# Moving one eighth of a gate projection from slot 11 to slot 19 in the last stick-breaking iteration

## The chip, the cores and the metric

The kernel runs on one core of one Trainium2 chip. The metric is the device time of one execution in microseconds; the time before is the median of 3 runs, 2171.8 us (2169.79 to 2174.42). Less is better.

## The reference, cut to what matters

One decoder layer on 1024 tokens of width 1024, all in float32. After an RMSNorm one input projection feeds two branches and two sigmoid gates:

```python
h = rms_norm(x, norm1_g)
proj = h @ w_in                      # sb_q, sb_k, sb_v, gla_q, gla_k, gla_v, gla_r, gla_lr, gate_sb, gate_gla
# (A) stick-breaking attention, 16 heads x 64, blocks of 128 queries
z = q @ k.T * scale                  # q, k normed per head
log_not = where(mask, log_sigmoid(-z), 0)
w = where(mask, exp(log_sigmoid(z) + reverse_cumsum_after(log_not)), 0)
o_sb = w @ v
# (B) gated linear attention -> o_gla
merged = sigmoid(gate_sb) * (o_sb @ w_branch_sb) + sigmoid(gate_gla) * (o_gla @ w_branch_gla)
x = x + merged @ w_out
x = x + (silu(h2 @ w_ffn_gate) * (h2 @ w_ffn_up)) @ w_ffn_down      # h2 = rms_norm(x)
```

The change is in (A), in its last pair of heads, beside which the last two tiles of 128 gate columns are computed.

## The kernel before, in words

The stages follow each other: norm and transpose, gated linear attention, stick-breaking attention, merging with the output projection, and the feed-forward part. Every float32 product is made of three matmuls of a high and a low part (high by high, low by high, high by low), so each operand is first rounded (`hi`) and the rest is kept (`lo`).

The stick-breaking stage (`stick_breaking`) takes two heads (one pair) in each of 8 iterations. An iteration is written out as 32 slots, and every engine walks the same slots in the same order, each with its own part of a slot's work. The parts meet through counting semaphores; nothing reorders them, so a wait holds all that stands behind it on its engine.

- Scores (`SCORE_SLOT`, 16 of them, n = 0 to 15, slots 0 to 7, 9 and 11 to 17). TensorE makes a block of 128 query rows in `z` (L612 to L615), ScalarE takes two sigmoids of it (L756 `rest`, L757 `beta`), VectorE scans one (L913), GpSimd multiplies the two into `rows` (L526). `rest` and `beta` have two buffers, so the sigmoids of score n wait for GpSimd's product of score n - 2.
- Weights (`WEIGHT_SLOT`, 24 of them, m = 0 to 23, slots 6 to 9 and 11 to 30). TensorE transposes a column of `rows` (L628) into bank `t`, ScalarE rounds it to `wt_hi` (L765), VectorE takes the rest `wt_lo` (L919), and one slot later TensorE multiplies both with `v` into `o` (`weigh`, L641 to L648). From `TAIL_STEP`, m = 13, on (slot 20) the odd m use bank `g0` and the transpose need not wait for the last `wt_lo`. After m = 3, 11, 15 and 23 ScalarE copies half of `o` (L770) and VectorE adds it up (L880); the next m waits for that sum. m = 11 is multiplied in slot 19, so m = 12 waits in slot 20 for the sum.
- Projection (`fill`, L149). A tile of 128 projected columns is made of 8 eighths of 6 matmuls each, four eighths for each half of the tokens. In iterations 1 to 7 a slot takes an eighth in each of the 32 slots. In the last iteration only two gate tiles are left, 16 eighths, and the list `LAST_FILL` gives their slots. After each fourth eighth, in the slot behind it, ScalarE takes the sigmoid of that half (`gate`, L732, into `sb_sq`), and the sync engine (SP) sends it to `gates_t` (L460). GpSimd splits the weight tile of step 6 in slot `LAST_FILL[7] + 2` and that of step 7 in slot `LAST_FILL[15] + 2` (L123 to L127), when the last reader of the buffer is done.
- Branch tiles. From slot 20 (`SPLIT_SLOT`) on, ScalarE and VectorE split one row block of the other branch's output per slot into `h_hi` and `h_lo` (L774, L924), and from slot 22 on TensorE multiplies 6 of them into `z` (L660). The blocks come through a ring of three buffers `og`, loaded by SP (L488), each load after the third waiting for the `h_lo` three blocks back.

SP takes its transfers in one written order. In the last iteration it is: two weight tiles, og blocks 0 to 2, the four gate halves (each waits for its `gate`), four loads `y<-osb_t` (L492), then og blocks 3 to 7 with three more y loads between them, and the output block after the last sum.

In the merging stage TensorE first finishes the last two branch tiles (L1760, `z`), then the eight of the other branch. A barrier stands between the stages.

Of the kernel before, what the change touches and what calls it, by code (L numbers as in the profile page):

```python
# [327 lines left out]
FIRST_UNITS = 4  # L328
LAST_GATES = 2
SB_TILES = FIRST_UNITS + 4 * (PAIRS - 1) + LAST_GATES  # L330
LAST_FILL = list(range(1, 12)) + list(range(14, 19))
TAIL_STEP = 13
MS_SLOT = [6, 10, 13, 17]
MS_AFTER = [10, 13, 17]
# [12 lines left out]
def stick_breaking(nc, c, hT, w_in, qk_gains, osb_t, gates_t, W, following, ot, ot_out, ot_read, ogla_t, z0, y, y_in):  # L347

    with ExitStack() as ctx:
# [75 lines left out]
        def slot_of_unit(s):  # L425
            return s // 8, s % 8
# [5 lines left out]
        with nc.Block() as block:  # L432
# [79 lines left out]
            def _(pool):  # L512
# [16 lines left out]
                def body(it, last):  # L529
# [3 lines left out]
                    if last:  # L533
                        splits = {0: (5, 0), LAST_FILL[7] + 2: (6, 1), LAST_FILL[15] + 2: (7, 2)}
                    else:
# [10 lines left out]
            def _(pe):  # L546
# [3 lines left out]
                def fill(it_units, step, eighth, use):  # L550

                    half, part = eighth // 4, eighth % 4
                    if eighth == 0:
                        W.take(pe, it_units, step)
                    if part == 0:
                        pe.wait_ge(g_free[half], use + 1)
                    ins = project_part(nc, G[half][:], W.tile(step), hT, half, part, 4)
                    if part == 3:
                        ins.then_inc(g_done[half], 1)
# [103 lines left out]
                def body(it, last):  # L663
                    for s in range(SLOTS):
# [9 lines left out]
                        if not last and s in SPREAD_SLOT and s not in SPREAD_AFTER:  # L674
                            spread(SPREAD_SLOT.index(s))
                        at = LAST_FILL.index(s) if last and s in LAST_FILL else s
                        u, eighth = slot_of_unit(at)
                        if s in LAST_FILL if last else u < 4:
                            fill(units(it), FIRST_UNITS + u, eighth, g_uses(it) + (u if last else (0, 2, 5, 6)[u]))
# [17 lines left out]
            def _(act):  # L697
# [30 lines left out]
                def gate(n_done, half, use):  # L728

                    act.wait_ge(g_done[half], use + 1)  # L730
                    act.wait_ge(gs_out, 16 * (NH * n_done + 1))
                    nc.scalar.activation(sq[:, half, :], G[half][:], ACT.Sigmoid).then_inc(g_free[half], 1)  # L732
# [43 lines left out]
                def body(it, last):  # L776
                    for s in range(SLOTS):
# [5 lines left out]
                        if not last:  # L783
# [13 lines left out]
                            if s == 28:  # L797
                                gate(it + 1, 0, g_uses(it) + 6)
                        elif s - 1 in LAST_FILL[3::4]:
                            i = LAST_FILL[3::4].index(s - 1)  # L800
                            gate(PAIRS + i // 2, i % 2, g_uses(it) + i // 2)
# [1577 lines left out]
```

## Time and profile before

| what | value |
|---|---|
| median of 3 runs | 2171.8 us (2169.79 to 2174.42) |
| profiled execution, its own time | 2174.0 us |
| its span | 2172.3 us |
| mean granted TensorE clock | 0.989 of full |
| TensorE matmul busy | 96% of the span |
| VectorE, ScalarE, GpSimd busy | 59%, 35%, 43% |
| last stick-breaking iteration | about 1134 to 1210 us of the span |

The span is what the profiler saw from the first instruction to the last; the execution's own time is 1.7 us longer. Times in rows are microseconds from the start of the span. Busy shares are means over stages with different limits, so the last iteration is read by itself.

### The profile page before, as it was taken

What the parts mean: (1) busy time and instruction counts of PE and PEld (TensorE: products, weight loads), DVE (VectorE), ACT (ScalarE), POOL (GpSimd) and SP (SyncE); (2) the same over time, 40 slices, a digit from 0 to 9 for tenths busy, and PEclk for the clock granted to TensorE, in tenths of its full rate; (3) what the DMA queues carried; (4) which work ended last, traced back from release to release, by engine and by line L of the source; (5) the groups of instructions that cost most, each with busy time, mean ns of one, the idle gap of its engine ahead of it and who ended that gap; (6) DMA issues with size and microseconds to landing.
All of it is one profiled execution on the core that took longest, in us unless ns stands there. A gap on an engine that the chain in (4) does not pass through costs nothing. (4 is left out here: it accounts for less than half of the span.)

```text
span 2172.3 us, 30125 instructions
## 1 busy us (share of the span) xinstructions
PE 2088.9 (96%) x10120; PEld 1705.2 (78%) x10120; DVE 1273.8 (59%) x1863; ACT 759.0 (35%) x1329; POOL 929.7 (43%) x817
## 2 busy tenths in 40 slices
PE   5999999999999999999998999996999999999999
PEld 4788888887777877787776788875888888888887
DVE  5558686852468568568667655658444444444444
ACT  3333342411346446445546300005323333232232
POOL 3323231323434434434435233326755555555552
PEclk8999999999999999999999999998999999999999
DMA  3211121222431431441543622211211111111112
GB/s 116 51 30 51 35 55 25 63 64 78 97 85 42 106 93 34 108 95 34 104 102 118 241 87 77 77 39 49 78 58 58 58 58 39 58 36 41 58 58 78
DMA packets 137777, 153.86 MB, mean 71 GB/s; under 512 B 7664, under 2 KB 112112, under 8 KB 137728
## 3 DMA queue, kind: packets, MB, share of 16 engines
q1 hardware_dynamic: 136000, 150.07, 25.3%
q10 hardware_dynamic: 1728, 3.15, 0.4%
q8 instruction: 29, 0.48, 0.1%
q14 instruction: 20, 0.16, 0.0%
HBM read 107.06 MB, written 20.97 MB: 59 GB/s over the span
## 5 line engine op out<-in xcount | busy, mean ns | idle before, releaser
L123 POOL TENSOR_TENSOR w_hi<-w_raw,w_ones 128x64 fp32r<-128x64 f32 x88 | 35.9, 408 | 680.0 <-PE gla_g L149 308.6
L526 POOL TENSOR_TENSOR sb_rows<-sb_beta,sb_rest 128x128 f32<-128x128 f32 (+7 forms) x128 | 154.3, 1206 | 226.5 <-DVE sb_rest L913 199.1
L127 POOL TENSOR_TENSOR w_lo<-w_raw,w_hi 128x512 fp32r<-128x512 f32 x176 | 239.5, 1381 | 7.3
L913 DVE TENSOR_TENSOR_SCAN sb_rest<-sb_rest 128x128 f32<-128x128 f32 (+7 forms) x128 | 210.0, 1640 | 39.2 <-ACT sb_beta L757 39.2
L919 DVE TENSOR_TENSOR sb_wt_lo<-sb_t,sb_wt_hi 128x512 fp32r<-128x512 f32 (+2 forms) x186 | 103.2, 555 | 123.8 <-ACT sb_wt_hi L765 121.7
L149 PE MATMUL sb_g<-h_hi,w_hi 128*128 128x512 f32 x544 | 155.1, 411 | 2.7 <-DVEq L816 1.9
L149 PE MATMUL sb_g<-h_lo,w_hi 128*128 128x512 f32 x544 | 150.8, 401 | 0.0
L149 PE MATMUL sb_g<-h_hi,w_lo 128*128 128x512 f32 x544 | 150.7, 401 | 0.0
L765 ACT CAST sb_wt_hi<-sb_t 128x512 fp32r<-128x512 f32 (+2 forms) x186 | 89.8, 483 | 167.0 <-PE sb_t L628 165.9
L149 PE MATMUL gla_g<-h_hi,w_hi 128*128 128x512 f32 x480 | 130.2, 407 | 6.2 <-DVEq L1377 6.2
L1924 POOL TENSOR_TENSOR ff_w_lo<-ff_raw_g,ff_w_hi 128x512 fp32r<-128x512 f32 x66 | 85.6, 1297 | 102.4 <-ACT ff_w_hi L2034 102.4
L149 PE MATMUL gla_g<-h_lo,w_hi 128*128 128x512 f32 x480 | 127.7, 399 | 0.0
L149 PE MATMUL gla_g<-h_hi,w_lo 128*128 128x512 f32 x480 | 126.3, 397 | 0.0
L149 PEld LDWEIGHTS sb_g<-h_lo,w_hi 128*128 128x128 f32 x544 | 97.8, 189 | 19.2
L149 PEld LDWEIGHTS sb_g<-h_hi,w_lo 128*128 128x128 f32 x544 | 97.9, 189 | 18.6
L2034 ACT CAST ff_w_hi<-ff_raw_g 128x512 fp32r<-128x512 f32 x66 | 41.1, 622 | 200.3 <-PE ff_a_u L2309 181.3
L149 PEld LDWEIGHTS gla_g<-h_hi,w_hi 128*128 128x128 f32 x480 | 89.0, 191 | 26.7 <-POOL w_lo L127 6.6
L149 PEld LDWEIGHTS sb_g<-h_hi,w_hi 128*128 128x128 f32 x544 | 94.1, 190 | 18.4 <-issue 2.5
L149 PEld LDWEIGHTS gla_g<-h_lo,w_hi 128*128 128x128 f32 x480 | 89.4, 189 | 20.4 <-issue 2.3
L628 PE MATMUL sb_t<-ident,sb_rows 128*128 128x128 f32 x560 | 93.7, 277 | 11.8 <-DVE sb_wt_lo L919 10.3
L1924 POOL TENSOR_TENSOR ff_w_lo<-ff_raw_u,ff_w_hi 128x512 fp32r<-128x512 f32 x66 | 86.6, 1312 | 42.9 <-ACT ff_w_hi L2034 42.9
L149 PEld LDWEIGHTS gla_g<-h_hi,w_lo 128*128 128x128 f32 x480 | 88.9, 188 | 18.0
(361 smaller groups left out, 5052.5 us busy)
## 6 DMA issues: line engine op xcount, KB each, us to landing
w_raw<-w_in SPq DMA_DIRECT2D x64, 512.0 KB, 8.2
ff_raw_g<-w_ffn_gate SPq DMA_DIRECT2D x11, 1024.0 KB, 5.4
ff_raw_u<-w_ffn_up SPq DMA_DIRECT2D x11, 1024.0 KB, 5.8
ff_raw_d<-w_ffn_down SPq DMA_DIRECT2D x11, 1024.0 KB, 4.8
sb_qs<-sb_q_st SPq DMA_DIRECT2D x32, 256.0 KB, 5.1
sb_kh<-sb_k_st SPq DMA_DIRECT2D x32, 256.0 KB, 5.0
sb_kl<-sb_k_st SPq DMA_DIRECT2D x32, 256.0 KB, 5.0
mp_sig<-gates_t SPq DMA_DIRECT2D x16, 512.0 KB, 4.3
```

Of the source, the lines that this page charges most:

```text
L123: self.nc.gpsimd.tensor_tensor(hi[:, 0:64], raw[:, 0:64], self.ones[:], ALU.mult)
L127: ins = self.nc.gpsimd.tensor_tensor(lo[:, at], raw[:, at], hi[:, at], ALU.subtract)
L149: ins = nc.tensor.matmul(acc, a[:, k, :], b[:, k, half * HALF:(half + 1) * HALF], start=(n == 0), stop=(n == len(steps) - 1))
L526: nc.gpsimd.tensor_tensor(rows[tb // 4][:, tb % 4, 0:width], beta[:, n % 2, 0:width], rest[:, n % 2, 1:width + 1], ALU.mult).then_inc(row_ ...
L628: ins = nc.tensor.transpose(bank[:, (tb - 4 * g) * P:(tb - 4 * g + 1) * P], rows[g][:, tb - 4 * g, j * P:(j + 1) * P], c["ident"][:])
L765: nc.scalar.copy(wt_hi[:, m % 2, a:HALF], weight_bank(m, last)[:, a:HALF]).then_inc(hi_ready, 1)
L913: nc.vector.tensor_tensor_scan(back, back, back, 1.0, ALU.mult, ALU.bypass).then_inc(scanned, 1)
L919: nc.vector.tensor_tensor(wt_lo[:, m % 2, a:HALF], weight_bank(m, last)[:, a:HALF], wt_hi[:, m % 2, a:HALF], ALU.subtract).then_inc(lo_rea ...
L1924: nc.gpsimd.tensor_tensor(w_lo[slot][:], operand(m, p), w_hi[slot][:], ALU.subtract).then_inc(w_ready, 1)
L2034: nc.scalar.copy(w_hi[slot][:], operand(m, p)).then_inc(w_high, 1)
```

## The change

The list of slots that take an eighth of the gate tiles in the last iteration is altered. Slot 11 no longer takes one, slot 19 does.

```diff
-LAST_FILL = list(range(1, 12)) + list(range(14, 19))
+LAST_FILL = list(range(1, 11)) + list(range(14, 20))
 TAIL_STEP = 13
```

What is derived from the list moves with it:

| | before | after |
|---|---|---|
| eighths 0 to 9 | slots 1 to 10 | the same |
| eighth 10 | slot 11 | slot 14 |
| eighths 11 to 15 | slots 14 to 18 | slots 15 to 19 |
| `gate` of half 0 and 1 of the first tile | slots 5 and 9 | the same |
| `gate` of half 0 and 1 of the second tile | slots 15 and 19 | slots 16 and 20 |
| GpSimd's split of tiles 6 and 7 | slots 10 and 20 | slots 10 and 21 |

The number of instructions, their shapes and their data are the same.

## Rows read from the trace of the kernel before

**Rows 1.** The page's busy times and shares.
```profile
PE 2088.9 (96%) x10120; PEld 1705.2 (78%) x10120; DVE 1273.8 (59%) x1863; ACT 759.0 (35%) x1329; POOL 929.7 (43%) x817
```
**Rows 2.** Timeline, slots 11 to 14: start, duration, engine, line, operation, idle before.
```profile
1160.94 0.66 PE L628 MATMUL sb_t<-ident,sb_rows 128*128 128x128 f32 x4 [1.14 <-POOL sb_rows L526]
...
1163.19 0.60 PE L628 MATMUL sb_t<-ident,sb_rows 128*128 128x128 f32 x4
...
1167.63 0.66 PE L628 MATMUL sb_t<-ident,sb_rows 128*128 128x128 f32 x4 [0.73 <-DVE sb_wt_lo L919]
...
1168.87 1.63 PE L149 MATMUL sb_g<-h_hi,w_lo 128*128 128x512 f32 x6
```
**Rows 3.** Timeline of VectorE, ScalarE and GpSimd in those slots.
```profile
1162.25 0.69 DVE L919 TENSOR_TENSOR sb_wt_lo<-sb_t,sb_wt_hi 128x512 fp32r<-128x512 f32 x1 [0.51 <-ACT sb_wt_hi L765]
...
1164.81 0.42 POOL L526 TENSOR_TENSOR sb_rows<-sb_beta,sb_rest 128x128 f32<-128x128 f32 x1
...
1165.33 0.58 ACT L756 ACTIVATE sb_rest<-z,sb_q_scale 128x384 f32<-128x384 f32 x1 [0.92 <-POOL sb_rows L526]
...
1166.89 0.69 DVE L919 TENSOR_TENSOR sb_wt_lo<-sb_t,sb_wt_hi 128x512 fp32r<-128x512 f32 x1 [1.11 <-ACT sb_wt_hi L765]
```
**Rows 4.** Timeline of all engines, slots 17 to 20.
```profile
1177.57 0.37 ACT L765 CAST sb_wt_hi<-sb_t 128x256 fp32r<-128x256 f32 x1
...
1181.42 3.27 DVE L913 TENSOR_TENSOR_SCAN sb_rest<-sb_rest 128x1024 f32<-128x1024 f32 x1
...
1183.03 0.60 ACT L732 ACTIVATE sb_sq<-sb_g 128x512 f32<-128x512 f32 x1
1183.66 0.58 ACT L770 COPY sb_o_low<-sb_o 64x512 f32<-64x512 f32 x1
...
1184.64 1.05 ACT L774 CAST h_hi<-sb_og 128x1024 fp32r<-128x1024 f32 x1
...
1184.76 2.00 POOL L526 TENSOR_TENSOR sb_rows<-sb_beta,sb_rest 128x1024 f32<-128x1024 f32 x1 [2.22 <-DVE sb_rest L913]
...
1185.19 0.67 DVE L880 TENSOR_TENSOR g_all<-sb_o,sb_o_low 64x512 f32<-64x512 f32 x1
...
1185.91 0.49 PE L641 MATMUL sb_o<-sb_wt_hi,sb_v 128*128 128x512 f32 x1 [2.88 <-DVE g_all L880]
```
**Rows 5.** Timeline of SP's issues (L460 gates, L492 y, L488 og).
```profile
1148.46 35.53 SPq L460 DMA_DIRECT2D gates_t<-sb_sq  x4
1184.10 1.81 SPq L492 DMA_DIRECT2D y<-osb_t  x4
1187.87 4.75 SPq L488 DMA_DIRECT2D sb_og<-ogla_t  x3
```
**Rows 6.** Timeline of ScalarE and VectorE, slots 23 to 27.
```profile
1194.75 1.05 ACT L774 CAST h_hi<-sb_og 128x1024 fp32r<-128x1024 f32 x1 [1.08 <-DMA sb_og<-ogla_t]
...
1195.83 1.23 DVE L924 TENSOR_TENSOR h_lo<-sb_og,h_hi 128x1024 fp32r<-128x1024 f32 x1 [1.33 <-ACT h_hi L774]
...
1204.68 1.05 ACT L774 CAST h_hi<-sb_og 128x1024 fp32r<-128x1024 f32 x1 [1.50 <-DMA sb_og<-ogla_t]
```
**Rows 7.** Timeline of TensorE, slots 25, 29 and the next stage's first matmul.
```profile
1197.71 0.50 PE L641 MATMUL sb_o<-sb_wt_hi,sb_v 128*128 128x512 f32 x1 [0.31 <-DVE sb_wt_lo L919]
...
1207.51 0.44 PE L641 MATMUL sb_o<-sb_wt_hi,sb_v 128*128 128x384 f32 x1 [2.09 <-DVE sb_wt_lo L919]
...
1211.49 0.76 PE L1760 MATMUL z<-h_hi,w_hi 128*128 128x512 f32 x1 [2.20 <-PEq L432]
```
**Rows 8.** Busy time by stretch; the last three columns: PEclk, DMA share, GB/s.
```profile
1139.10:1142.50 3.40, 1.91 (x9) 1.27 (x8) 0.49 (x1) 1.58 (x4) 2.32 (x4) 1.00 0.65 187
1183.50:1186.90 3.40, 0.99 (x6) 0.76 (x7) 3.40 (x5) 2.14 (x5) 2.14 (x2) 1.00 0.96 194
1186.90:1193.70 6.80, 6.16 (x20) 4.77 (x19) 5.91 (x6) 3.60 (x6) 6.42 (x4) 0.50 0.90 359
...
1211.50:1217.60 6.10, 6.10 (x14) 4.75 (x15) 5.05 (x5) 6.10 (x7) 0.00 (x0) 0.50 0.78 255
```

## The prediction, made before the changed kernel had run

> **What bounds the kernel now.** I read the page first. TensorE is busy 96% of the span [rows 1], so what an edit is worth is what it gives to or takes from TensorE's order of work, and the whole sum is read in the last iteration. There I went through TensorE's timeline for its idle gaps, then at each gap through the engine that ended it, then through SP's issues, and last through the clock by stretch.
>
> The reader is to see four things. First, slot 11 is not a place where TensorE sets the pace: its transposes waited 1.14 us for GpSimd, and two and three slots on it waits again, the last time 0.73 us, for `wt_lo` [rows 2]. Second, slot 20 has a hole of 2.88 us, ended by VectorE's sum [rows 4]. Third, that hole and what follows did not cost what they seem to: from slot 23 on the pace is a DMA's. ScalarE waits 1.08 us for og block 3, and from its landing a fixed train runs: 1.05 us for `h_hi`, 1.23 us for `h_lo`, `wt_lo`, and TensorE at 1197.71, after a wait of its own [rows 6, 7]. Block 7 does it once more: ScalarE waits 1.50 us, TensorE 2.09 us [rows 6, 7]. Fourth, the y loads that stand ahead of block 3 in SP's order were issued at 1184.10, directly behind the last gate half, whose sigmoid ended at 1183.63 (1183.03 + 0.60) [rows 4, 5]. The DMA engines were busy 0.96 and 0.90 of the time from there to 1193.7 [rows 8].
>
> **The change part by part.**
>
> *Slot 11 loses six matmuls.* Six take 1.63 us in a row, and about 1.4 us of pace (the last overlaps what follows) [rows 2]. What comes earlier? The transposes of slot 12 stood at 1163.19; the `wt_lo` they need ended at 1162.94 (1162.25 + 0.69) [rows 2, 3]. So at most 0.2 us is won, and TensorE then idles 1.1 us. Even this is lost: the sigmoids of slot 12 waited for GpSimd's product, which ended at 1165.23 (1164.81 + 0.42) behind a weight split that this change does not move. They began at 1165.33, two of them take till 1166.3, ScalarE's rounding and `wt_lo` follow until 1167.58, and the transposes of slot 14 start at 1167.63 [rows 2, 3]. None of these hangs on the removed matmuls. Bounds: 0 to -0.2 us; I take 0.
>
> *Slots 14 to 18.* Each has an eighth as before, only another one. Cost 0 on TensorE. The gate of half 0 goes one slot down on ScalarE, from before the transposed column of slot 16 to before that of slot 17: the cast that stood at 1177.57 comes 0.5 us later (a gate takes 0.60, overlapping its neighbour), and with it the `wt_lo` and a scan. VectorE's next thing, the scan of 3.27 us at 1181.42, hangs on later work that has the room; 0.1 us may be left. 0 to +0.5 us; I take +0.1.
>
> *Slot 19 gains six matmuls, 1.4 us.* They stand before the `weigh` of m = 11, in a stretch where TensorE then had 2.88 us to wait [rows 4]. TensorE reaches slot 20's wait at 1184.5 instead of 1183.03. The `weigh` of m = 11 ends at about 1184.1, the copy of half of `o` follows at 1184.2 instead of 1183.66 and ends at 1184.8, before VectorE is free for the sum at 1185.19: its 3.27 us scan ran to 1184.69, and 0.5 us of `wt_lo` stands between [rows 4]. So the sum is as late as before. The cover holds by 0.4 us; were it gone, the cost would be the 1.4 us. 0 to +0.5; I take +0.1, that of the line above and not a second one.
>
> *The last gate half.* This is the term that I think decides. In the order before, ScalarE took it at 1183.03, ahead of the copy of `o`. Now it is in slot 20, behind that copy (to 1184.8) and behind the cast of m = 13, whose transposes end at about 1184.6; the cast takes 0.4, so the gate runs from 1185.2 to 1185.75. Against 1183.63 that is 2.1 us later. Behind it on ScalarE stands `h_hi` of block 0, at 1185.75 instead of 1184.64 [rows 4]; `h_lo` of block 0, one cast and TensorE's `weigh` of m = 14 come some 0.3 to 0.5 us later, all ahead of the wait for block 3. Behind it on SP stand the four y loads and then blocks 3 to 5: the y loads go at 1186.2, and block 3 at about 1188.2 instead of 1187.87 [rows 5]. Block 3 is hardly issued later. But its bytes queue behind the four y loads of 512 KB, and they begin 2.1 us later on DMA engines that had been without work. Its landing, 1194.7 before [rows 6], is then 1196.8. The bounds: +1.0 if the slow beginning of those loads (194 GB/s in the first 3.4 us against 359 afterwards [rows 8]) does not come again at the later time, and +2.3. I take +2.1, as nothing in the rows ties the slow start to a place in time.
>
> By the Trainium skill (DMA: Bandwidth & Descriptors, Queues, rings and completion order) each DMA engine takes descriptors in ring order within the queue of one issuing engine, and it round-robins only between different queues. All of these loads are SP's. Were it round-robin among them, block 3 would land nearly as before and this term would be 0.3 us.
>
> *Behind block 3.* `h_lo` of block 3 and 4 release the issues of blocks 6 and 7; so block 7, the later wait of 1.50 us [rows 6], keeps its distance to block 3 and shifts by the same 2.1 us. The slack that would take it up is not there: both waits hold TensorE.
>
> *GpSimd's split* in slot 21 instead of 20: nothing of GpSimd's lies between, and it was busy with the last product until 1186.76 (1184.76 + 2.00) [rows 4], while the last eighth ends at 1183.8. Cost 0.
>
> *The clock.* After the hole of 2.88 us the granted clock was 0.50, that is 1.2 GHz, from 1186.9 to 1193.7 [rows 8]. In the new order the hole is 1.5 us; a gap of 1.49 us at 1140.5 (idle in the stretch with 1.91 busy of 3.40) was followed by no fall [rows 8]. So this fall likely goes. It wins nothing: TensorE only comes earlier to the wait for block 3, and idles there for some 3 us. That gap calls the clock down again right behind it, where the 7.6 us of work before the wait for block 7 (1197.71 + 7.6 = 1205.3, then 2.09 idle) would take some 3.5 us more, of which the idle hides 2.1: +1.4 us if it happens. Against it, the wait for block 7 shrinks, and with it the idle ahead of the merging stage, whose first 6.1 us ran at 0.50 after the gaps of 2.09 and 2.20 us [rows 7, 8]: a fall avoided there gives back 3.05 us, with a chance of about one half. The two nearly cancel; I take 0 and keep -3.1 to +1.8.
>
> The Trainium skill (TensorE: Matmul & The Clock Gate, Part 1) says that the activity monitor runs free and does not start with the kernel. So which of several like gaps is followed by a fall may differ between executions; the runs before differ by 4.6 us, but no row shows that this is why.
>
> *Sum.* 0 + 0.1 + 2.1 + 0 = +2.2 us, less the 0.1 that may be hidden behind the landing: +2.1. The profiled execution had 2174.0 us, span 2172.3 and 1.7 around it, 2.2 above the median of the runs. On its own time the sum gives 2176.1, on the median of 2171.8 it gives 2173.9 us.
>
> **The rivals.**
>
> *A second fall of the clock, behind slot 11.* The new 1.1 us of idle in slot 11 comes directly behind the 1.14 us that is there [rows 2], 2.2 us together, between the 1.49 us that brought no fall and the 2.88 us that did [rows 4, 8]. For it: the sum. Against it: it is broken by transposes and a score, and the hole of 2.88 us was in one piece. Price: slots 12 to 14 have 5.5 us of TensorE work in 6.6 us; at half clock they would push slot 14 by about 1.7 us (5.5 more, less what the chain through GpSimd and the two waits hide, and a return of the clock in slot 14), and from 1167.63 to slot 16 TensorE works without a gap, so it goes through to everything behind. 2173.9 + 1.7 = 2175.6, and with +1.4 of the clock in the tail 2177.0: slower.
>
> *Faster: the clock in the merging stage.* If the idle ahead of it shrinks below what brings the clock down, its first 6.1 us take 3.05. This decides once the idle left ahead of it is nearer to the 1.49 us that brought no fall than to the 2.09 and 2.20 us that did. With the late loads it gives 2173.9 - 3.1 = 2170.8; if the landing of block 3 is not late either (the slow start gone and the issue order kind) 2168.7. For it: TensorE will be the later one at block 7. Against it: the 2.20 us of the barrier stay in any case.
>
> *The loads are hidden.* Block 3 lands as before, since its own issue is hardly later. Then nothing is left but the 0.1: 2171.9. Against it: 0.96 busy DMA engines.
>
> **How the numbers follow.** The forecast 0.62, the second fall 0.18, the faster clock 0.12, the hidden loads 0.08. This kernel's measurement can tell about 0.2%, 4.3 us, from no change: under 2167.5 is faster, over 2176.1 slower. Slower takes two thirds of the second fall and 0.06 of the forecast (the tail's +1.4 to +1.8 on top of 2.3): 0.18. Faster takes a third of its case: 0.04. Same 0.78. The range goes from 2169.8 (the clock's gift with a part of the late loads) to 2177.6 (second fall with the tail's).
>
> **What would show it.** In the changed profile: TensorE idle before slot 12's transposes, about 1.1 us; slot 14's transposes as far behind slot 11's as before (6.7 us); the hole in slot 20 about 1.5 us and no half clock right after it; the gate's sigmoid behind the copy of `o`; four y loads 2.1 us later relative to the last scan; ScalarE waiting for block 3 about 3 us; the next stage's first matmul 50.55 + 2.1 = 52.7 us behind slot 11's transposes at 1160.94. Wrong would be: slot 14 earlier, or block 3 landing no later, or a total under 2169.8.

## The result, and the profile after

The changed kernel took 2175.94 us in the median of 20 runs (2171.59 to 2182.15), the kernel before 2172.76 us in 20 runs of the same sessions. The ratio is 1.0015 with a 95% interval of 1.0009 to 1.0021, about 3.3 us slower (2.0 to 4.6): under the 0.2% that was set as the border, but clear of noise. The forecast was 2173.9 us, +2.1, in a range of 2169.8 to 2177.6.

The profiled execution of the changed kernel took 2173.8 us with a span of 2172.1, not more than the 2174.0 and 2172.3 of the one before. Single executions of one kernel lie up to 11 us apart, and TensorE's granted clock goes with that: of the 20 of the changed kernel the longest had the lowest mean clock, 0.984, and the shortest one of the highest, 0.991 (before slot 11 alone the profiles of this study differ by 7 us). So the profiles are compared by distances inside the last iteration. All times in rows are from the start of the span; slot 11's transposes stand at 1160.94 in the kernel before [rows 2] and at 1161.77 after, so 0.83 is to be taken off.

Slots 11 to 14 of the changed kernel, the timeline of TensorE and then of the other engines (start, duration, engine, line, idle before):

```profile
1161.77 0.66 PE L628 MATMUL sb_t<-ident,sb_rows 128*128 128x128 f32 x4 [1.16 <-POOL sb_rows L526]
...
1163.83 0.66 PE L628 MATMUL sb_t<-ident,sb_rows 128*128 128x128 f32 x4 [1.09 <-DVE sb_wt_lo L919]
...
1168.44 0.66 PE L628 MATMUL sb_t<-ident,sb_rows 128*128 128x128 f32 x4 [0.84 <-DVE sb_wt_lo L919]
...
1165.62 0.42 POOL L526 TENSOR_TENSOR sb_rows<-sb_beta,sb_rest 128x128 f32<-128x128 f32 x1
...
1166.13 0.58 ACT L756 ACTIVATE sb_rest<-z,sb_q_scale 128x384 f32<-128x384 f32 x1 [1.03 <-POOL sb_rows L526]
...
1167.69 0.69 DVE L919 TENSOR_TENSOR sb_wt_lo<-sb_t,sb_wt_hi 128x512 fp32r<-128x512 f32 x1 [1.11 <-ACT sb_wt_hi L765]
```

The eighth that left slot 11 became idle time: 1.09 us appear ahead of slot 12, where there was none. Slot 12 stands 2.06 us behind slot 11 instead of 2.25, and slot 14 6.67 us behind it instead of 6.69 [rows 2]. It is held by the same train, GpSimd's product, the sigmoids, `wt_lo` [rows 3]. The removal won nothing.

Slots 19 and 20:

```profile
1183.10 1.64 PE L149 MATMUL sb_g<-h_hi,w_lo 128*128 128x512 f32 x6
...
1186.72 0.51 PE L641 MATMUL sb_o<-sb_wt_hi,sb_v 128*128 128x512 f32 x1 [1.47 <-DVE g_all L880]
...
1182.23 3.27 DVE L913 TENSOR_TENSOR_SCAN sb_rest<-sb_rest 128x1024 f32<-128x1024 f32 x1
...
1186.00 0.67 DVE L880 TENSOR_TENSOR g_all<-sb_o,sb_o_low 64x512 f32<-64x512 f32 x1
...
1184.94 0.58 ACT L770 COPY sb_o_low<-sb_o 64x512 f32<-64x512 f32 x1 [0.98 <-PE sb_o L641]
1185.55 0.48 ACT L765 CAST sb_wt_hi<-sb_g 128x384 fp32r<-128x384 f32 x1
1185.92 0.60 ACT L732 ACTIVATE sb_sq<-sb_g 128x512 f32<-128x512 f32 x1
1186.41 1.05 ACT L774 CAST h_hi<-sb_og 128x1024 fp32r<-128x1024 f32 x1
```

The hole of 2.88 us is 1.47 us, and VectorE's scan and sum stand where they stood (less 0.83: 1181.40 and 1185.17, against 1181.42 and 1185.19 in [rows 4]). The last gate half stands behind the copy and the cast, at 1185.09 on the old clock instead of 1183.03.

SP's issues (the last row is that of block 7), and ScalarE, VectorE and TensorE at blocks 3 and 7:

```profile
1158.72 28.16 SPq L460 DMA_DIRECT2D gates_t<-sb_sq  x3
1186.99 1.82 SPq L492 DMA_DIRECT2D y<-osb_t  x4
1188.85 4.66 SPq L488 DMA_DIRECT2D sb_og<-ogla_t  x3
...
1201.45 0.33 SPq L488 DMA_DIRECT2D sb_og<-ogla_t  x1
...
1197.39 1.04 ACT L774 CAST h_hi<-sb_og 128x1024 fp32r<-128x1024 f32 x1 [4.71 <-DMA sb_og<-ogla_t]
...
1198.46 1.23 DVE L924 TENSOR_TENSOR h_lo<-sb_og,h_hi 128x1024 fp32r<-128x1024 f32 x1 [3.99 <-ACT h_hi L774]
...
1206.77 0.59 ACT L765 CAST sb_wt_hi<-sb_t 128x512 fp32r<-128x512 f32 x1 [0.75 <-PE sb_t L628]
1207.26 1.05 ACT L774 CAST h_hi<-sb_og 128x1024 fp32r<-128x1024 f32 x1
...
1200.35 0.79 PE L641 MATMUL sb_o<-sb_wt_hi,sb_v 128*128 128x512 f32 x1 [3.27 <-DVE sb_wt_lo L919]
...
1210.10 0.44 PE L641 MATMUL sb_o<-sb_wt_hi,sb_v 128*128 128x384 f32 x1 [0.47 <-DVE sb_wt_lo L919]
...
1214.09 0.77 PE L1760 MATMUL z<-h_hi,w_hi 128*128 128x512 f32 x1 [2.20 <-PEq L432]
```

Against [rows 5 to 7], less 0.83: y loads +2.06, issue of block 3 +0.15, its landing and `h_hi` +1.81, TensorE behind it +1.81, behind block 7 +1.76, the next stage +1.77. ScalarE's wait of 1.08 us has become 4.71 us, and TensorE's of 0.31 us has become 3.27 us.

Busy time by stretch (the last three columns are the granted clock, the DMA share and GB/s):

```profile
1183.50:1186.90 3.40, 1.93 (x12) 1.42 (x11) 3.40 (x4) 2.40 (x5) 1.33 (x1) 1.00 0.00 0
1186.90:1193.70 6.80, 5.61 (x31) 4.21 (x31) 6.43 (x7) 4.16 (x7) 6.72 (x5) 1.00 0.94 279
...
1200.40:1203.70 3.30, 3.30 (x8) 2.52 (x9) 2.76 (x3) 1.02 (x2) 0.00 (x0) 0.50 0.91 326
1214.10:1217.40 3.30, 3.30 (x8) 2.62 (x9) 2.26 (x2) 3.30 (x4) 0.00 (x0) 0.50 0.58 189
```

The half clock from 1186.9 to 1193.7 [rows 8] is gone. It has come back behind the wait for block 3, at 1200.4, and there TensorE's work is on the path. Block 7 took 4.6 us from its issue at 1201.45, so it had landed at 1206.1; in the kernel before it took 5.8 us from 1198.82 and landed at 1204.7. Less the 0.83 that is 0.6 us later. ScalarE had waited 1.50 us for it [rows 6]. Now it waits for TensorE's transposes (the 0.75 us at 1206.77) and takes block 7 1.2 us after it has landed. So the +1.77 at the next stage is 0.6 us of late loads and about 1.2 us of work at half clock. TensorE's 0.47 us at 1210.10 is not a wait for a load any more, as the 2.09 us [rows 7] were. Another fall stands at the next stage. It was 3.4 us long here and 6.8 us in the kernel before.

### The profile page after: what moved, and what is told of

It reads as the page before. It is cut to its first block and busy times, and to the rows that moved or that the text cites. A ratio compares the mean times of both kernels' runs of the same rounds, so it can differ in the third digit from the quotient of the medians.

```text
span 2172.1 us, 30125 instructions
## 1 busy us (share of the span) xinstructions
PE 2087.0 (96%) x10120; PEld 1703.3 (78%) x10120; DVE 1274.2 (59%) x1863; ACT 758.6 (35%) x1329; POOL 929.6 (43%) x817
## 5 line engine op out<-in xcount | busy, mean ns | idle before, releaser
L123 POOL TENSOR_TENSOR w_hi<-w_raw,w_ones 128x64 fp32r<-128x64 f32 x88 | 36.0, 409 | 681.2 <-PE gla_g L149 308.3
L919 DVE TENSOR_TENSOR sb_wt_lo<-sb_t,sb_wt_hi 128x512 fp32r<-128x512 f32 (+2 forms) x186 | 103.2, 555 | 123.3 <-ACT sb_wt_hi L765 121.2
```

The source lines that it names most:

```text
L123: self.nc.gpsimd.tensor_tensor(hi[:, 0:64], raw[:, 0:64], self.ones[:], ALU.mult)
L919: nc.vector.tensor_tensor(wt_lo[:, m % 2, a:HALF], weight_bank(m, last)[:, a:HALF], wt_hi[:, m % 2, a:HALF], ALU.subtract).then_inc(lo_rea ...
```

## The experiments

Each was timed beside the kernel before. A time of 11 or 12 runs is known to about 0.1% (2 us). The distance inside one profile, from the `wt_lo` of slot 11 (m = 4, L919) to the next stage's first matmul, is finer, but it is that of one execution. It is 1211.49 - 1162.25 = 49.24 us in the kernel before. Where an edit adds lines, line numbers in rows are higher by up to four.

| kernel | distance, us | against before | ratio of times | 95% interval |
|---|---|---|---|---|
| changed | 51.01 | +1.77 | 1.0015 | 1.0009 to 1.0021 |
| after_again | 51.33 | +2.09 | 1.0013 | 1.0004 to 1.0021 |
| old_fill_gate_late | 50.21 | +0.97 | 1.0011 | 1.0000 to 1.0021 |
| gate_ahead_of_copy | 49.63 | +0.39 | 1.0001 | 0.9991 to 1.0011 |
| fill_19_for_18 | 50.29 | +1.05 | 1.0020 | 1.0011 to 1.0029 |
| fill_12_for_11 | 50.44 | +1.20 | 1.0012 | 1.0003 to 1.0021 |
| old_fill_y_first | 46.28 | -2.96 | 0.9991 | 0.9980 to 1.0002 |
| new_fill_y_first | 47.50 | -1.74 | 0.9996 | 0.9988 to 1.0005 |
| old_fill_og_first | 46.24 | -3.00 | 1.0001 | 0.9992 to 1.0010 |
| new_fill_og_first | 46.49 | -2.75 | 1.0004 | 0.9995 to 1.0012 |
| old_fill_late_split | 45.69 | -3.55 | 1.0005 | 0.9994 to 1.0015 |
| new_fill_late_split | 45.38 | -3.86 | 0.9985 | 0.9976 to 0.9994 |

The distance also stops about where the next fall of the clock begins, and that fall lasted 3.4 us in six of the profiles (both of the changed kernel, `old_fill_gate_late`, `fill_19_for_18`, `old_fill_og_first`, `new_fill_late_split`) and 6.8 us in the other seven, the kernel before among them. Measured to an instruction of VectorE some 20 us further on (L1717, at 1230.93 in the kernel before) the changed kernel is only 0.45 and 0.83 us behind in its two profiles, and `old_fill_gate_late` and `fill_19_for_18` are 0.31 and 0.21 us ahead. So the profiles show where the time goes up to the next stage. That a kernel is slower as a whole rests on the timed runs.

**The place of the last gate.** The changed slots, the gate taken one slot sooner (`gate_ahead_of_copy`), and the old slots with the gate one slot later and nothing else moved (`old_fill_gate_late`):

```diff
 # both: the slots of the four gate halves are a list
+LAST_GATE = [5, 9, 16, 19]    # gate_ahead_of_copy, on the changed LAST_FILL
+LAST_GATE = [5, 9, 15, 20]    # old_fill_gate_late, on the old LAST_FILL
-                        elif s - 1 in LAST_FILL[3::4]:
-                            i = LAST_FILL[3::4].index(s - 1)
+                        elif s in LAST_GATE:
+                            i = LAST_GATE.index(s)
```

> The changed slots, but ScalarE takes the last gate half in slot 19, ahead of the copy of o, instead of in slot 20 behind it and behind the cast of m = 13. Theory (the last gate's send holds the y loads, and they hold og block 3): the gate can run as soon as the eighth in slot 19 ends, some 1.2 us sooner than in the changed kernel, so the y loads and block 3 are 0.9 us late against the kernel before instead of 2.1; time +0.9 to +1.5 us over before, where the changed kernel had +3.2. Rival (the clock: one more fall of TensorE's clock from the new idle of 1.1 us in slot 11): the slot is as idle as in the changed kernel, so the time stays at +3.2. Rival (the matmuls in slot 19 themselves delay the sum of o): as in the changed kernel, +3.2.

> The kernel before, its eighths in the old slots, but the last gate half taken in slot 20 behind the copy of o and the cast of m = 13. Theory of the send: the gate then starts at about 1184.15 instead of 1183.03, the y loads and block 3 come 1.1 us later, and so does the next stage: +1.1 us. Both rivals: no matmul is moved, so 0.

ScalarE (gate, copy, wait for block 3) and SP (y loads) in the first:

```profile
1185.54 0.60 ACT L733 ACTIVATE sb_sq<-sb_g 128x512 f32<-128x512 f32 x1 [0.81 <-PE sb_g L149]
1186.16 0.58 ACT L771 COPY sb_o_low<-sb_o 64x512 f32<-64x512 f32 x1
...
1196.94 1.05 ACT L775 CAST h_hi<-sb_og 128x1024 fp32r<-128x1024 f32 x1 [3.53 <-DMA sb_og<-ogla_t]
...
1206.20 1.05 ACT L775 CAST h_hi<-sb_og 128x1024 fp32r<-128x1024 f32 x1 [0.82 <-DMA sb_og<-ogla_t]
...
1186.60 1.82 SPq L493 DMA_DIRECT2D y<-osb_t  x4
```

In the second, with TensorE's clock behind the wait for block 3 (0.50, third column from the end):

```profile
1190.21 0.60 ACT L733 ACTIVATE sb_sq<-sb_g 128x512 f32<-128x512 f32 x1
...
1201.82 1.04 ACT L775 CAST h_hi<-sb_og 128x1024 fp32r<-128x1024 f32 x1 [3.29 <-DMA sb_og<-ogla_t]
...
1191.27 1.82 SPq L493 DMA_DIRECT2D y<-osb_t  x4
...
1205.90:1209.30 3.40, 3.40 (x12) 2.61 (x11) 1.84 (x3) 0.77 (x2) 0.00 (x0) 0.50 1.00 367
```

Counted from the `wt_lo` of slot 11 the y loads stand at 21.85 us before, 23.91 changed, 23.21 here in the first (1186.60 - 1163.39) and 22.93 in the second (1191.27 - 1168.34); ScalarE takes block 3 at 32.50, 34.31, 33.55 and 33.48. The second is the clean one: no matmul is moved, the loads come 1.08 us late and block 3 0.98. Its profile gave +0.97 where +1.1 was expected, its time agrees without settling it. The first gave back 1.4 of the 1.77 us in the profile, and its time is that of the kernel before. That is less loss than the +0.9 to +1.5 expected, though its loads were 1.36 us late and not 0.9. The rivals, that slot 11 or slot 19 carries the loss by itself, would have kept it at +3.2; the upper end of its interval is +2.4.

The two also part the loads from the clock. Block 3 is about 1 us late in both. In the first TensorE waited 2.10 us for it, no fall followed, block 7 landed 0.4 us late and the next stage is 0.39 us late. In the second it waited 2.48 us, the half clock followed, and the next stage is 0.97 us late although block 7 (4.7 us from its issue at 1205.88) landed no later than in the kernel before. From taking block 3 until it was free for block 7 ScalarE needed 8.4 us in the first (1206.20 - 0.82 - 1196.94) and 9.9 in the changed kernel (1207.26 - 1197.39), where the clock fell. So in these profiles a late block 3 reaches the next stage in full only through the clock behind it.

**Slot 19 without slot 11, and slot 12 for slot 11.**

```diff
-LAST_FILL = list(range(1, 12)) + list(range(14, 19))
+LAST_FILL = list(range(1, 12)) + list(range(14, 18)) + [19]         # fill_19_for_18
+LAST_FILL = list(range(1, 11)) + [12] + list(range(14, 19))         # fill_12_for_11
```

> The kernel before with its last eighth in slot 19 instead of 18; slot 11 keeps its eighth. The last gate half is taken in slot 20, as in the changed kernel. Theory of the send: the y loads come 2.1 us late and the next stage 1.8 to 2.1 us later behind slot 11; no fall of the clock behind slot 11; timed +1.8 to +3. Rival (slot 11's idle and the clock carry the loss): next stage and time as before.

```profile
1186.43 0.61 ACT L732 ACTIVATE sb_sq<-sb_g 128x512 f32<-128x512 f32 x1
...
1197.39 1.04 ACT L774 CAST h_hi<-sb_og 128x1024 fp32r<-128x1024 f32 x1 [3.36 <-DMA sb_og<-ogla_t]
...
1187.50 3.10 SPq L492 DMA_DIRECT2D y<-osb_t  x4
```

Beside the gate GpSimd's split moves here, to slot 21, but it began as far behind slot 11 as before. With slot 11 untouched the kernel is slower, 1.0020 of the time before: the loss needs nothing of slot 11. The y loads came 1.82 us late (1187.50 - 1163.83 - 21.85), but block 3 only 1.06 (1197.39 - 1163.83 - 32.50), near the lower end of +1.0 that the prediction had set. So from the lateness of the loads to that of block 3 between 0.1 and 0.8 us can be lost, and the profile's +1.05 is less than was expected. Its time was not less, about +4.3 us. The mean granted clock of its 11 timed runs is 0.9870, against 0.9885 in the 27 of the kernel before beside them, so the time holds more half clock than the kernel before. Whether the edit brought it is not shown. In its profile the hole of slot 20 is 1.74 us, with a wait of 0.96 us at 1183.23 ahead of it, and the half clock followed from 1187.8 on, as it did not behind the holes of 1.47 and 1.52 us of the changed kernel.

> The kernel before with the eighth of slot 11 in slot 12 instead; gates, splits and SP as before. Theory: slot 12 waits for GpSimd and VectorE as slot 11 does; slots 11 to 13 have room for an eighth in any place, so slot 14 stands as before, or up to 0.8 us late if slot 12's work makes the transposes of slot 13 late, and 0.2 us of that is left in the end; timed 0 to +0.8. If slot 11 were on the path, this would be faster by up to 1.4.

This expectation missed. The clock fell right behind slot 11, and slot 12's eighth ran under it:

```profile
1163.58 1.11 PE L628 MATMUL sb_t<-ident,sb_rows 128*128 128x128 f32 x4 [1.08 <-DVE sb_wt_lo L919]
...
1165.43 1.76 PE L149 MATMUL sb_g<-h_lo,w_hi 128*128 128x512 f32 x4
...
1169.96 0.66 PE L628 MATMUL sb_t<-ident,sb_rows 128*128 128x128 f32 x4 [0.34 <-DVE sb_wt_lo L919]
```

Slot 14 came 8.44 us behind slot 11 (at 1161.52) instead of 6.69, and all else with it. Slot 12 at full clock was not seen, so the part about its room stays open.

**The changed kernel again.**

> The changed kernel once more, unaltered, beside the others on one chip. In its first profile the next stage began 1.76 us later behind slot 11 than in the kernel before, and the 20 timed runs said +3.2. Theory (the send of the last gate, with a size that depends on where TensorE's clock falls): the distance from slot 11 to the next stage is again +1.8 us, or more, up to +3.5, if the clock falls for longer in the work between the waits for blocks 3 and 7; timed +2 to +4. Rival of the clock in slot 11: a fall right behind slot 11 and slot 14 more than 1 us late.

The profile repeats the first (+2.09, timed 1.0013), with a fall behind the wait for block 3 (3.44 us) once more and block 7 taken 1.2 us after its landing. Here the clock did fall behind slot 11. The same stretch of both kernels, the first row this one, the second `old_fill_og_first`, whose slot 11 has its eighth:

```profile
1164.60:1168.00 3.40, 3.40 (x12) 1.91 (x12) 1.49 (x3) 2.23 (x4) 2.18 (x3) 0.50 0.00 0
```

```profile
1164.60:1168.00 3.40, 3.07 (x19) 1.71 (x16) 1.33 (x2) 2.00 (x5) 2.53 (x4) 1.00 0.00 0
```

Of the seven profiles with slot 11 empty five have such a fall (this one, gate_ahead_of_copy, fill_12_for_11, new_fill_og_first, new_fill_late_split), of the six with it filled none. Its price, at the end of the last scan, was 0.16 us here and 0.44 to 0.55 in the other three that leave slot 12 empty too: it lasts 3.4 us, and the waits behind it hide most.

**SP's order.** The four y loads do not need the gate. They were put ahead of the last send (`old_fill_y_first`, `new_fill_y_first`), then the later three behind all og blocks as well (`old_fill_og_first`, `new_fill_og_first`):

```diff
 # y_first: inside the loop over the four sends
+                        if n == LAST_GATES - 1 and half == NH - 1:
+                            sp.wait_ge(z_done, NSC * PAIRS)
+                            for k in range(4):
+                                load_ahead(k)
                         send_gate(half, g_uses(PAIRS - 1) + n, (PAIRS - 1 + n) * P)
-                sp.wait_ge(z_done, NSC * PAIRS)
-                for n in range(4):
-                    load_ahead(n)
 # og_first, besides
                 for i in range(BRANCH_RING, KT):
                     load_branch(i)
-                    if i > 4:
-                        load_ahead(i - 1)
+                for i in range(5, KT):
+                    load_ahead(i - 1)
```

> The kernel before, but SP issues the four y loads ahead of the last gate half, as soon as the last scores are done (about 1178.5 on the clock of the trace before, 5.6 us sooner). Theory of the send: block 3 then lands some 3.5 us after its own issue at 1187.9, by 1191.5 instead of 1194.7; the waits of 0.31 and 2.09 us of TensorE in slots 25 and 29 go, and the next stage starts 2 to 2.4 us sooner; -2 to -2.5 us, and up to 3 us more in executions in which the clock then doesn't fall ahead of the merging stage. Both rivals: the loads were hidden, 0.

> The changed slots with the same order of SP. Theory of the send: the lateness of the last gate no longer holds anything, and now the shorter hole in slot 20 and the full clock after it count: the wait for block 3 (3.27 us in the changed kernel) and that for block 7 go, the next stage starts 3.5 to 5 us sooner than in the kernel before; -3.5 to -6 us, and faster than the old slots with the same order by 1 to 2.5. Rival of the clock (slot 11): still a fall more often, so slower than the old slots with the same order. Rival of slot 19: slower than the old slots with the same order by 1.4 or more.

> The kernel before with the four y loads ahead of the last gate half, and the later three y loads behind all og blocks. With only the first of the two the next stage began 2.97 us sooner behind slot 11, and TensorE still waited 0.83 us for block 7, ahead of which y loads stood. Theory of the send and the queue: that wait goes too, the next stage starts 3.5 to 3.9 us sooner than before; timed -2 to -4. Rival (the loads are not what TensorE waits for): as with the first alone.

> The changed slots with both changes of SP's order. With the first alone TensorE waited 1.47 us for block 7, and 1.03 us in slot 24 for VectorE's sum. Theory: with the loads out of the way VectorE is next, whose scan, two roundings' rests and three h_lo beside GpSimd's split run without a gap from slot 18 to 24 in either kernel; so the filled hole gives nothing either, and the next stage starts where it does with the old slots in the same order, within 0.5 us. Rival (the hole was worth its 1.4 us once the loads are gone): 1 to 1.5 us sooner than the old slots in this order.

SP and TensorE's waits in `old_fill_y_first`:

```profile
1185.78 1.76 SPq L492 DMA_DIRECT2D y<-osb_t  x4
1190.87 0.34 SPq L460 DMA_DIRECT2D gates_t<-sb_sq  x1
1195.09 4.76 SPq L488 DMA_DIRECT2D sb_og<-ogla_t  x3
...
1193.13 0.54 PE L642 MATMUL sb_o<-sb_wt_hi,sb_v 128*128 128x512 f32 x1 [2.88 <-DVE g_all L881]
...
1200.86 0.49 PE L642 MATMUL sb_o<-sb_wt_hi,sb_v 128*128 128x512 f32 x1 [0.42 <-DVE g_all L881]
...
1211.74 0.44 PE L642 MATMUL sb_o<-sb_wt_hi,sb_v 128*128 128x384 f32 x1 [0.83 <-DVE sb_wt_lo L920]
```

The loads go 5.52 us sooner (16.33 instead of 21.85 behind slot 11's `wt_lo`), the wait for block 3 is gone, and the next stage starts 2.96 us sooner, more than the 2 to 2.4 us that were expected. With that the lateness of the gate holds none of SP's loads. The expectation that the filled hole would then win 1 to 2.5 us missed: the new slots stood 1.2 us behind the old ones, with TensorE waiting 1.03 us in slot 24 for VectorE's sum and 1.47 us for block 7. That block was issued at the same distance in both kernels and landed 1.0 us later in the new slots; why is open. With the og blocks first the two stood within 0.25 us, as expected. But the later y loads behind the blocks won nothing: `old_fill_og_first` was expected 3.5 to 3.9 us sooner and came 3.00, as with the first edit alone (2.96), although TensorE's wait at block 7 went from 0.83 to 0.47 us. The times of these four moved less than the distances, 0.9991 to 1.0004, and `old_fill_og_first` not at all, which is outside what its 3.0 us would give; `new_fill_y_first` too missed its expected -3.5 to -6 us. A profile is one execution, and the timed ones can differ in where the clock falls: the hole of 2.88 us is still in `old_fill_og_first`, and with the loads away a fall behind it is on the path. That fall lasted 3.4 us in this profile and 6.8 us in that of the kernel before. That this is the reason is argued, not shown.

**GpSimd's split held back.** VectorE's `h_lo` of blocks 1 and 2 took 1.81 and 2.09 us beside GpSimd's split of the last weight tile. Both kernels have SP's two edits; the new slots also have the gate in slot 19.

```diff
                         if s in splits:
                             step, uses = splits[s]
+                            if last and step == 7:
+                                pool.wait_ge(og_low, KT)
                             W.split(pool, units(it), step, (g_done[1], g_uses(it) + uses))
```

> The kernel before with the y loads ahead of the last gate half, the later ones behind all og blocks, and GpSimd's split of the last weight tile held until VectorE's last h_lo. In the order without the late split the next stage came 3.0 us sooner behind slot 11. Theory: what is left from slot 20 to 24 is VectorE, whose h_lo of blocks 1 and 2 took 1.81 and 2.09 us beside the split and 1.23 us without it; they fall to 1.23 us each, and the next stage comes another 0.5 to 1.5 us sooner, 3.5 to 4.5 in all. Rival (GpSimd's work is beside the path): -3.0 as without it.

> The changed slots with the same three edits and the last gate half taken in slot 19 ahead of the copy of o. Theory: with VectorE's chain shorter and the loads away, the filled hole can give something: the next stage 4 to 5.5 us sooner behind slot 11 than in the kernel before, up to 1 us better than the old slots with the same edits; less, if the clock falls behind slot 11. Rival: VectorE's sum in slot 20 still sets the pace, equal to the old slots.

VectorE's `h_lo` 0 to 2, GpSimd's split, and TensorE's waits in `new_fill_late_split`:

```profile
1187.87 1.23 DVE L928 TENSOR_TENSOR h_lo<-sb_og,h_hi 128x1024 fp32r<-128x1024 f32 x1 [0.29 <-ACT h_hi L778]
...
1189.50 1.23 DVE L928 TENSOR_TENSOR h_lo<-sb_og,h_hi 128x1024 fp32r<-128x1024 f32 x1
...
1190.84 1.22 DVE L928 TENSOR_TENSOR h_lo<-sb_og,h_hi 128x1024 fp32r<-128x1024 f32 x1
...
1204.00 0.32 POOL L123 TENSOR_TENSOR w_hi<-w_raw,w_ones 128x64 fp32r<-128x64 f32 x1 [15.99 <-DVE h_lo L928]
...
1187.16 0.50 PE L645 MATMUL sb_o<-sb_wt_hi,sb_v 128*128 128x512 f32 x1 [1.49 <-DVE g_all L884]
...
1189.49 0.38 PE L645 MATMUL sb_o<-sb_wt_hi,sb_v 128*128 128x256 f32 x1 [0.91 <-DVE sb_wt_lo L923]
...
1204.45 0.44 PE L645 MATMUL sb_o<-sb_wt_hi,sb_v 128*128 128x384 f32 x1 [0.47 <-DVE sb_wt_lo L923]
```

The `h_lo` fell to 1.23 us, and the waits in slots 24 and 25 are gone. The old slots gained 0.55 us of distance on their order without it, at the low end of what was expected. The new ones gained 1.11, which holds the sooner gate as well as the held split; they ended 3.86 us ahead of the kernel before, just short of the 4 to 5.5 expected. `new_fill_late_split` is the only kernel with an interval below 1: 0.9985 (0.9976 to 0.9994), median 2168.25 us, against 2172.04 of the kernel before beside it. The old slots with the same edits timed 1.0005 although their distance is but 0.31 us longer. The mean granted clock of their 11 timed runs is 0.9875 against 0.9895 in the new slots. So the new slots are the better ones once the loads, the sends and the split are out of the way, and the gain looks like the clock. That it is the clock behind the filled hole is not shown, since these means are over the whole span.

## Why the prediction was right

The direction and the start of the mechanism were right: the last gate late, the y loads behind it late, block 3 late. The time lies in the range. From block 3 to the next stage the working was not right, and there two errors made up for each other: that is luck.

*Slot 11, taken at 0.* Right: 6.67 for 6.69 us. *The hole, covered.* Right: 1.47 us for 1.5, VectorE's sum unmoved (1185.17 for 1185.19). *Slots 14 to 18, +0.1.* The scan stood within 0.02 us; nothing.

*The last gate half, +2.1.* The issue was met: y loads +2.06, and +2.17 in the repetition (24.02 behind slot 11's `wt_lo`). The landing of block 3 was +1.81 and +2.09; in the two profiles with a late gate and slot 11 as before it was 0.98 for 1.08, and 1.06 for 1.82. The slow beginning of the loads comes again, but not always whole. The prediction saw nothing that ties it to a place. The runs tie it to the gate's send right ahead: the first y load took 5.0 us to land in the kernel before, 5.1 in the changed one, 4.9 in `new_fill_y_first`, where a gate's send stood 0.5 us ahead of it too, and 3.3 in `old_fill_y_first`, where SP had sent nothing for 4 us. The ring order (the Trainium skill, DMA: Bandwidth & Descriptors, Queues, rings and completion order) agrees with it: block 3 was issued 0.15 us later and landed 1.8 us later, behind the loads ahead of it.

*Behind block 3, the same 2.1 us.* Wrong. Block 7 did not keep its distance: its issue was 1.8 us later, but it landed only 0.6 us later, and 0.9 in the repetition, and nothing waited for it. With the clock up, an estimate from these rows is +0.6 us at the next stage, as `gate_ahead_of_copy` has +0.39 with block 7 landed 0.4 us late.

*The clock, taken at 0.* The forecast of two places held in both profiles: no fall behind the smaller hole, one behind the wait for block 3. For the fall ahead of the merging stage the prediction gave one half; it was there, 3.4 us long instead of 6.8. The cost behind block 3 was about 1.2 us (block 7 taken at 1207.26, landed at 1206.1), near the +1.4 that the prediction had named and set against the gift of the merging stage. So the +1.77 came out as 0.6 and 1.2 where the sum had 2.1 and 0.

The profiles have +1.8 and +2.1 at the next stage, the timed runs +3.3 (2.0 to 4.6) and +2.8 (0.9 to 4.6). Behind the next stage 1.3 us are given back in both profiles, so a remainder of 1 us or more is not settled. The timed runs do not point to more half clock: the mean granted clock of the repetition's 11 runs is 0.9885, that of the 35 of the kernel before beside them 0.9881. What can still differ is where the falls lie, and the timed runs do not show that.

*The second fall, 0.18 and 1.7 us.* Both numbers were wrong, in opposite ways. It came in five of seven profiles with slot 11 empty (one of the changed kernel's two) and cost 0.16 to 0.55 us, except where slot 12 had been filled: there slot 14 was 1.75 us late. I had the return of the clock too late and did not credit the waits behind it. Of the other two rivals the hidden loads are out for block 3 (each kernel with late loads took it later), and nearly right for block 7. The changed kernel was not faster, but the shorter fall in the merging stage was there in its profiles.

ScalarE waited 4.71 us for block 3 where about 3 us had been named as a sign; TensorE's wait was the 3.27 us.

## What to carry to other kernels

A piece of work moved into an engine's idle time carries its readers along. Ask what is queued behind each of them, the DMA issues above all: here a gate that nobody needed soon stood ahead of loads, and behind them came the block that TensorE waited for ten microseconds later. Before filling a hole look at what bounds the stretch behind it, since a gap ahead of another engine's wait only moves, and the longer wait can bring the clock down. The only kernel that came out faster had the filled hole, and the loads, the sends and VectorE's neighbour out of the way. A sum that comes out right is not yet a mechanism: look at each waypoint of it.

## What the runs showed of the hardware

VectorE and GpSimd slowed each other: `h_lo` of 1024 columns took 1.23 us alone and 1.81 and 2.09 us beside the split, and 1.23 us again once the split was held back. GpSimd's first instruction of the split (L123) took 1.30 us beside `h_lo` and 0.32 us held back.

Loads that SP issued 0.4 to 0.5 us behind a gate's send began slowly: the first landed 4.3 to 5.3 us after its issue in ten profiles, and 3.2 to 3.3 us in the three in which the last send was 4 us away.

The hole of 2.88 to 2.91 us in slot 20 was followed by the half clock within 2.5 us of its end in all six profiles that have it, for 6.8 us in one and 3.4 in five. The holes of 1.47 to 1.52 us were not followed by it in any of six; the one of 1.74 us, with 0.96 us of idle ahead of it in slot 18, was.

Idle of 1.16 and 1.09 us, with 1 us of work between, was followed by the half clock (1.2 GHz) in some executions and not in others of the same program (the changed kernel's two profiles). The Trainium skill (TensorE: Matmul & The Clock Gate, Part 1) says that the monitor runs free of the kernel's start; these two profiles agree with it.
